# Expert stage of a hybrid decoder layer: token rows gathered as quarters and turned by VectorE, index copies on VectorE

## The reference

```python
def hier_moe(h, ...):                     # h: 2048 x 1024
    # top-1 of 4 groups, top-2 of the 8 experts in it: two assignments and two gates per token
    # assignments sorted by expert, each expert's rows padded to blocks of 128 (MOE_BLOCK)
    def expert_block(args):
        xb, e = args                      # xb: 128 rows of h, e: their expert
        hid = jax.nn.silu(xb @ w_gate[e]) * (xb @ w_up[e])   # 1024 -> 512
        return hid @ w_down[e]                               # 512 -> 1024
    out = lax.map(expert_block, (rows.reshape(n_blocks, 128, -1), block_e)).reshape(n_rows, -1)
    return segment_sum(out[dest] * gate, token)
```

## Time and profile before

| | |
|---|---|
| median of 3 runs | 2221.45 us |
| the runs | 2222.25, 2213.61, 2221.45 us |
| profiled execution: time / span | 2212.72 / 2211.1 us |
| busy: PE, PEld, DVE, ACT, POOL | 90%, 76%, 64%, 49%, 24% |
| TensorE clock granted, mean over the span | 0.954 |
| blocks in the expert stage (gate matmuls 392, eight per block and kind) | 49 |
| expert stage, from the first gate matmul to the last down split | 1244 to 2143 us of the span |

### The profile page before, as it was taken

The page is one execution under the profiler, slowest core; times in us unless marked ns, Lnnn a source line. Parts: engine busy times, 40 slices in busy tenths (PEclk is TensorE's granted clock), DMA queues, the critical chain, the costliest instruction groups (busy, mean ns, idle before and its releaser), DMA issues. The chain is left out here.

```text
span 2211.1 us, 32053 instructions
## 1 busy us (share of the span) xinstructions
PE 1996.7 (90%) x10153; PEld 1672.5 (76%) x10154; DVE 1415.3 (64%) x2368; ACT 1072.4 (49%) x1591; POOL 525.4 (24%) x637
## 2 busy tenths in 40 slices
PE   6999999886898988969996699999999999999970
PEld 5887888785687878858885588888888888888860
DVE  4675687466797887945556675675568755546344
ACT  4322211224377787753223364665567655545433
POOL 2000111241000000000000254454445545344430
PEclk9999999998899999989997699999999999999995
DMA  8675986835435323024335588797889978667637
GB/s 263 218 228 196 327 288 223 262 133 124 123 69 125 76 69 67 1 84 167 134 134 200 196 309 281 255 331 273 283 277 387 348 268 304 188 229 238 218 85 314
DMA packets 170121, 458.37 MB, mean 207 GB/s; under 512 B 19872, under 2 KB 69104, under 8 KB 144432
## 3 DMA queue, kind: packets, MB, share of 16 engines
q1 hardware_dynamic: 122896, 285.30, 37.4%
q0 software_dynamic: 31008, 138.37, 20.5%
q10 hardware_dynamic: 16128, 33.56, 4.3%
HBM read 342.08 MB, written 115.10 MB: 207 GB/s over the span
## 5 line engine op out<-in xcount | busy, mean ns | idle before, releaser
L2215 DVE TENSOR_TENSOR w_down_lo<-w_down_raw,w_down_hi 128x2048 fp32r<-128x2048 f32 x64 | 144.1, 2289 | 124.5 <-ACT w_down_hi L2152 123.0
L2299 PE MATMUL m_bank<-w_down_hi,hidden_T_hi 128*128 128x512 f32 x392 | 160.4, 409 | 6.8 <-DVE w_down_lo L2215 6.8
L2215 DVE TENSOR_TENSOR w_gate_lo<-w_gate_raw,w_gate_hi 128x2048 fp32r<-128x2048 f32 x63 | 141.6, 2289 | 38.8 <-ACT w_gate_hi L2152 32.4
L2278 PE MATMUL m_bank<-w_gate_hi,rows_T_hi 128*128 128x512 f32 x392 | 156.5, 399 | 6.4 <-DVE rows_T_lo L2220 3.9
L2278 PE MATMUL m_bank<-w_up_hi,rows_T_hi 128*128 128x512 f32 x392 | 158.8, 405 | 0.0
L2279 PE MATMUL m_bank<-w_gate_lo,rows_T_hi 128*128 128x512 f32 x392 | 156.1, 398 | 0.0
L2280 PE MATMUL m_bank<-w_gate_hi,rows_T_lo 128*128 128x512 f32 x392 | 156.0, 398 | 0.0
L2215 DVE TENSOR_TENSOR w_up_lo<-w_up_raw,w_up_hi 128x2048 fp32r<-128x2048 f32 x64 | 146.2, 2287 | 15.1 <-ACT w_up_hi L2152 15.1
L2300 PE MATMUL m_bank<-w_down_lo,hidden_T_hi 128*128 128x512 f32 x392 | 155.4, 396 | 0.0
L2280 PE MATMUL m_bank<-w_up_hi,rows_T_lo 128*128 128x512 f32 x392 | 154.8, 395 | 0.0
L2279 PE MATMUL m_bank<-w_up_lo,rows_T_hi 128*128 128x512 f32 x392 | 154.5, 394 | 0.0
(11 more groups left out here) (424 smaller groups left out, 5288.3 us busy)
## 6 DMA issues: line engine op xcount, KB each, us to landing
w_gate_raw<-in_w_gate_dram SPq DMA_DIRECT2D x64, 1024.0 KB
w_down_raw<-in_w_down_dram POOLq DMA_DIRECT2D x64, 1024.0 KB
w_up_raw<-in_w_up_dram SPq DMA_DIRECT2D x64, 1024.0 KB, 8.2
hT_d<-hT_parts SPq DMA_DIRECT2D x32, 512.0 KB, 5.2
hT_parts<-hT_d SPq DMA_DIRECT2D x32, 512.0 KB, 9.0
k_parts<-kT_d SPq DMA_DIRECT2D x64, 256.0 KB, 8.5
u_tok<-in_x_dram SPq DMA_DIRECT2D x16, 512.0 KB, 5.8
qT_d<-qk_out ACTq DMA_DIRECT2D x32, 256.0 KB, 3.8
```

Of the source, the lines that this page charges most:

```text
L2215: dve.tensor_tensor(wlo[w][:, halves[i]], raw[w][:, halves[i]], whi[w][:, halves[i]], ALU.subtract).then_inc(lo_done[w], 1)
L2278: pe.matmul(to[:], xh[:, k], whi[w][:, c], start=k == 0, stop=False)
L2299: pe.matmul(DN[h][:], hh[:, k], whi[2][:, part(k)], start=k == 0, stop=False)
```

## The change

A block's rows are gathered by four indirect DMAs in place of one. `h2` is seen as 1 KB quarter rows, and the DMA number `r` fills columns `256r` to `256r+255` of `rows_in`: partition `32f+i` gets quarter `f` of the token in slot `32r+i`. VectorE then turns 32x32 blocks (`turn`, two instructions of 128x512), which puts column numbers on partitions and slots along the free axis, in the new SBUF tile `rows_T`. The high and low parts of the rows are made from this tile. Blocks 0 and 1 keep the old way.

TensorE loses the 8 transposes of each iteration and the wait for `x_in`, and gets, once, four small matmuls that spread the token numbers over the partitions (`PI`). VectorE gets, once, `part_rows`, and in each iteration two `turn`, one `part_index`, two `slot_index` and waits for `x_in`, `out_st` and `gate_in`. GpSimd loses all index copies and two of its three small adds. ScalarE's wait for `u_done` moves ahead of the rows' high parts, which now wait for `turned`.

```diff
+    def pause(self, pool, ones, by=1):
+        pool.tensor_tensor(self.paused[:], ones[:, 0:1], ones[:, 1:2], ALU.add).then_inc(self.pauses, by)
+
+    def gather_parts(self, pool, d):
+        for r in range(PARTS):
+            pool.indirect_dma_start(self.x[:, r * PART:(r + 1) * PART], None, d["h2"].rearrange("r (f c) -> (r f) c", f=PARTS),
+                                    bass.IndirectOffsetOnAxis(ap=self.part_idx[:, r:r + 1], axis=0)).then_inc(self.x_in, 16)
...
             def _(pool):
-                def gather_gate(b, count):
-                    pool.tensor_copy(gate_idx[:], gate_ids[:, bass.ds(b, 1)]).then_inc(gate_set, 1)
-                    pool.wait_ge(gate_set, count)
-                    pool.tensor_tensor(hold[:], ones[:, 0:1], ones[:, 1:2], ALU.add)
+                def gather_gate():
                     pool.indirect_dma_start(gate[:], None, d["gates"], ...).then_inc(gate_in, 16)
-                def add_rows(b, count, used):
+                def add_rows(set_by, used, pauses):
+                    pool.wait_ge(store.pauses, pauses)
+                    pool.wait_ge(slot_ready, set_by)
                     pool.wait_ge(d_used, used)
-                    pool.tensor_copy(to_idx[:], ids[:, bass.ds(b, 1)]).then_inc(to_set, 1)
-                    pool.wait_ge(to_set, count)
-                    pool.tensor_tensor(hold[:], ones[:, 0:1], ones[:, 1:2], ALU.add)
+                    store.pause(pool, ones)
                     pool.indirect_dma_start(d["x1"], ..., out[:], None, compute_op=ALU.add).then_inc(out_st, 16)
...
                 with pool.Fori(0, later(pool) - 1) as j:
-                    pool.wait_ge(xT_psum, 2 * j + 6)
-                    gather(j + 3)
-                    add_rows(j, j + 1, 2 * j + 4)
-                    gather_gate(j + 1, j + 2)
+                    pool.wait_ge(store.pauses, 2 * j + 2)
+                    pool.wait_ge(turned, 2 * j + 2)
+                    pool.wait_ge(part_ready, j + 2)
+                    store.pause(pool, ones)
+                    store.gather_parts(pool, d)
+                    add_rows(2 * j + 3, 2 * j + 4, 2 * j + 3)
+                    gather_gate()
                     # the down weights' loads follow, as before
...
             # ScalarE
+                def rows_hi(h, want):
+                    act.wait_ge(turned, want)
+                    act.activation(xh[:, 4 * h:4 * h + 4], xT[:, 4 * h:4 * h + 4], ACT.Copy).then_inc(xh_done, 1)
...
-                    rows_hi(0, 2 * j + 5)
-                    rows_hi(1, 2 * j + 6)
+                    act.wait_ge(u_done, j + 2)
+                    rows_hi(0, 2 * j + 1)
+                    rows_hi(1, 2 * j + 2)
                     with where_below(nc, act, now, order):
-                        act.wait_ge(u_done, j + 2)
                         split_hi(1, order, 0)
                     out_half(0, j)
...
             # VectorE
+                def rows_lo(h, want):
+                    dve.wait_ge(xh_done, want)
+                    dve.tensor_tensor(xl[:, 4 * h:4 * h + 4], xT[:, 4 * h:4 * h + 4], xh[:, 4 * h:4 * h + 4],
+                                      ALU.subtract).then_inc(xl_done, 1)
+                def turn(h):
+                    dve.transpose(xT[:, 4 * h:4 * h + 4].rearrange("p k (r i) -> p r k i", r=PARTS),
+                                  x[:].rearrange("p (r j k) -> p r k j", r=PARTS, k=KT)[:, :, 4 * h:4 * h + 4]).then_inc(turned, 1)
+                def part_rows():
+                    # memset; copies into pick (128x512), ids_f (128x64), quad_i; shift; copy into quad
+                    dve.wait_ge(part_psum, 1)
+                    dve.tensor_scalar(part_ids[...], PI[...], float(PARTS), quad[:, 0:1], ALU.mult, ALU.add).then_inc(part_set, 1)
+                    dve.wait_ge(part_set, 1)
+                    part_index(2)
+                def part_index(b):
+                    dve.tensor_copy(store.part_idx[:], part_ids[:, bass.ds(b * PARTS, PARTS)]).then_inc(part_ready, 1)
+                def slot_index(b, of_rows):
+                    # one copy of 128x1 into to_idx (of_rows) or gate_idx, then_inc(slot_ready, 1)
...
                 split_lo(1, 0, 1)
+                part_rows()
                 split_lo(2, 0, 0)
                 split_lo(2, 0, 1)
...
                         split_lo(0, order, 1)
+                    dve.wait_ge(x_in, 64 * j + 96)
+                    dve.wait_ge(xl_done, 2 * j + 4)
+                    turn(0)
+                    turn(1)
+                    part_index(j + 3)
                     hidden(j + 1)
                     rows_lo(0, 2 * j + 5)
                     rows_lo(1, 2 * j + 6)
+                    dve.wait_ge(out_st, 16 * j + 16)
+                    slot_index(j, True)
+                    dve.wait_ge(gate_in, 16 * j + 16)
+                    slot_index(j + 1, False)
...
             # TensorE
                 product(G, 0, g_done)
+                pe.wait_ge(pick_set, 2)
+                for r in range(PARTS):
+                    last = pe.matmul(PI[:, r * NBLK:(r + 1) * NBLK], pick[:, r].rearrange("p f i -> p (f i)"), ids_f[:], start=True, stop=True)
+                last.then_inc(part_psum, 1)
...
                     product(U, 1, u_done)
-                    pe.wait_ge(x_in, 16 * j + 48)
-                    rows_T(0)
-                    rows_T(1)
                     down(j, before)
```

More of the change, by code:

```diff
@@ L43 @@
 NBLK = 64
+PARTS = 4
+PART = D // PARTS
+QUAD = P // PARTS
 MIN_BLK = 2 * SEQ // P
@@ L2056, in source, with experts @@
         return a[("w_gate", "w_up", "w_down")[w]][0, e].rearrange("o (p k) n -> p (o k n)", k=k)[:, self.halves[i]]
-def experts(nc, ident, ones, ids, gate_ids, meta, store, a, d):
+def experts(nc, ident, ones, const, ids, gate_ids, meta, store, a, d):
     with ExitStack() as ctx:
@@ L2063, in experts @@
         sem = ctx.enter_context(phase_semaphores(nc))
-        bank = [ctx.enter_context(nc.psum_tensor(f"m_bank{i}", [P, BANK], F32)) for i in range(7)]
-        G, U, XT, HT, DN = bank[0], bank[1], bank[2:4], bank[4], bank[5:7]
+        bank = [ctx.enter_context(nc.psum_tensor(f"m_bank{i}", [P, BANK], F32)) for i in range(8)]
+        G, U, XT, HT, DN, PI = bank[0], bank[1], bank[2:4], bank[4], bank[5:7], bank[7]
         FT = FF // P
@@ L2076, in experts @@
         x_in = store.x_in
-        gate_in, to_set, gate_set = (sem(n) for n in ("slot_gate_in", "to_idx_set", "gate_idx_set"))
+        gate_in, part_ready, slot_ready = (sem(n) for n in ("slot_gate_in", "part_idx_set", "slot_idx_set"))
         g_done, u_done, d_done, silu_done, hid_done = (sem(n) for n in ("g_done", "u_done", "d_done", "silu_done", "hid_done"))
-        xT_psum, xh_done, xl_done, hT_psum = (sem(n) for n in ("rT_psum", "rT_hi_done", "rT_lo_done", "hidT_psum"))
+        xT_psum, turned, xh_done, xl_done, hT_psum = (sem(n) for n in ("rT_psum", "rows_turned", "rT_hi_done", "rT_lo_done", "hidT_psum"))
+        pick_set, part_psum, part_set = (sem(n) for n in ("row_of_quad_set", "part_ids_psum", "part_ids_set"))
         with nc.Block() as block:
@@ L2139, in _ @@
                 end = later(pool)
-                add_rows(end - 1, end, 2 * end + 2)
-                gather_gate(end, end + 1)
-                add_rows(end, end + 1, 2 * end + 4)
+                add_rows(2 * end + 1, 2 * end + 2, 2 * end)
+                gather_gate()
+                add_rows(2 * end + 2, 2 * end + 4, 2 * end + 1)
                 final = place(pool, end - 1)
@@ L2230, in hidden_lo @@
                     dve.tensor_tensor(hl[:], HT[:].rearrange("p (k t) -> p k t", k=FT), hh[:], ALU.subtract).then_inc(hl_done, 1)
+                slot_index(0, False)
                 split_lo(0, 0, 1)
                 split_lo(1, 0, 0)
[L2234 to L2235 removed]
+                first_rows_lo(0, 1)
+                first_rows_lo(1, 2)
                 split_lo(1, 0, 1)
+                part_rows()
                 split_lo(2, 0, 0)
@@ L2264, in _ @@
                 end = later(dve)
+                dve.wait_ge(out_st, 16 * end + 16)
+                slot_index(end, True)
                 hidden_lo(end + 2)
@@ L2447, in hybrid_layer @@
             route(nc, ident, ones, logits, const, ids, gate_ids, meta, store, a, d)
-            experts(nc, ident, ones, ids, gate_ids, meta, store, a, d)
+            experts(nc, ident, ones, const, ids, gate_ids, meta, store, a, d)
         finish(nc, a, d, out)
```

52 lines of the change are left out of this document (36 added, 16 removed).

## The result

| | before | after |
|---|---|---|
| median | 2214.41 us (5 runs) | 2233.91 us (5 runs: 2232.27 to 2241.92) |
| profiled execution: time / span | 2212.72 / 2211.1 us | 2233.5 / 2231.9 us |
| gathers of rows, mean of one | 1.04 us x49 | 1.56 us x192 and one whole |

The ratio is 1.0084, with a 95% interval of 1.0057 to 1.0111: slower by 0.8%, where 2193 was forecast and 2223 was the end of the range. All ratios here are of undisturbed executions; one each of e1 and e2, and one of the kernel before beside them, took 2896 to 4100 us and is left out of its ratio.

A forecast was written before the change was run, and what follows sets the result against it. PE was taken as sole limit in 34 iterations, with three resources nearly as long in full ones. The terms -38.9 + 5.0 + 4.0 + 3.0 - 0.3 gave -27 us; forecast 2193 us, range 2176 to 2223.

The forecast's parts named there:

- TensorE's transposes: Row transposes leave PE's stream in 48 iterations: 0.81 us each, 38.9 us in all, a block passing in 17.34 us.
- The turn at 0.60 us: Each 128x512 turn on VectorE was priced like a subtraction of its shape: 0.60 us, bounds 0.30 to 1.20.
- The room in gate-and-up iterations: Slack before the next gate product: 2.68 us, 0.5 left after the change, hiding turns up to 0.85 us each.
- rival 2: Slow turns of 1.2 us lengthen gate-and-up and full iterations: -9 us in all, 2212; chance 0.13.
- first turn 0.60: The one turn counted in VectorE's 10.03 us part of the full iterations' loop, at 0.60 us.
- ScalarE's order: Rows' high parts wait for the turn, closing a 17.9 us loop in nine full iterations: +5.0 us.
- GpSimd and DMA, +4 us: Late down loads from four gathers, together with full DMA in full iterations: +4 us, bounds 0 and 18.
- uncovered: about 1 us: Down loads issued 4.2 us later but wanted 3 us later in full iterations, leaving about 1 us uncovered.
- The rule on two SBUF operands: VectorE instructions with two SBUF inputs delay GpSimd: two gathers, some 1.2 us more before down loads; left out.
- The start, +3.0: The index table waits for TensorE before the first down splits, delaying the second expert: +3.0 us, bounds 2 and 6.
- Rival 3: GpSimd's gathers and add, pausing for VectorE's splits, become the full iterations' loop: about +32 us, 2253; chance 0.15.
- the prediction's signs of being wrong: Turns over 0.85 us, four 2.8 us gathers with PE idle over 2, VectorE awaiting `x_in`, or clock below 1.00.

The follow-up runs named there:

- e1: The changed kernel with each VectorE turn cut to half of its columns; 2215.68 us, 0.9998 of the kernel before.
- e2: The changed kernel with one gather of whole rows in place of four of quarters; 2212.51 us, 0.9990 of the kernel before.
- e13: The changed kernel with turns reading neighbouring columns and the loop's low parts taking their second operand from a zeroed PSUM bank; 2186.78 us.
- e5: The changed kernel with turns that read 32 neighbouring columns in place of every eighth; 2207.91 us.
- e9: The changed kernel with the loop's weight low parts taking a PSUM bank of zeros as second operand instead of the high part; 2211.07 us.
- e10: The changed kernel with a second, reordered copy of h2 stored and gathered, so turns read neighbouring columns and results are kept; 2214.33 us.
- e3: The changed kernel with half turns and one gather of whole rows; 2189.23 us, 0.9881 of the kernel before.
- e7: The changed kernel with turns and index copy ahead of the gate splits and part of the index table's making behind the first down splits; 2235.66 us.

## Why the prediction was wrong, step by step

From the first gate product to the last lie 47 of the 48 blocks, so its sum there was -26.1 (-38.1 + 5.0 + 4.0 + 3.0); measured was +16.0. The gap of 42 us, by the kinds of interval: full 21.3 (forecast -11.3 + 9.0 = -2.3, measured +19.0), gate and up 13.5 (-13.0, +0.5), down only 7.1 (-13.0, -5.9), start 0.4. Taking both wrong prices away (e13) gave back 19.9, 14.9 and 7.2.

- *TensorE's transposes, 0.81 us a block:* right. The interval without splits is 17.23 us after, forecast 17.34; gate-and-up ones too, once the turn is short (17.25).
- *The turn at 0.60 us:* the first failed step. It is 1.17 (e5: 0.69 when it reads neighbouring columns), at the upper bound of 1.20. The choice went by the shape of the nearest row, a subtraction that reads neighbours; the stride was named as what speaks for 1.20, and then outweighed. The room in gate-and-up iterations was worked out as enough for 0.85 a turn; with 1.17 they are 0.8 us over 17.34 (rival 2 had 0.6). In the loop of the full iterations the prediction counted one turn, "first turn 0.60". At 1.17 both stand in it: the first on DVE, the second as ACT's wait of 0.45 us between the two rows' high parts (1677.00 above). In the run of six, behind its first, e9 with the long turns has intervals of 18.90 to 18.98 us, e13 with the short ones mostly 17.95: 0.95 us, twice the 0.48. The mean of all full intervals got 0.76 shorter (e10).
- *ScalarE's order, a loop of 17.9 us:* right in mechanism and size where both prices are taken away: 17.95 in e13, with ACT's and DVE's parts as worked out. (e3's 17.97 is a mean over blocks of 17.27 to 19.15 us and comes near it by chance.)
- *GpSimd and DMA, +4 us:* the second failed step. The place was right: the down loads were put at 12.9 us behind the gate product, and came at 10.4 to 14.0, 13.3 ahead of the longest block. What they cost was not: "uncovered: about 1 us". In a run of full iterations they land at 1684.4 and 1689.0, 11.0 and 15.0 us after their issue, ACT waits 4.3 us, and the interval is 23.76 us. Two of the 14 are like this (the other took 23.88), and the nine that follow a full one have a mean of 20.3 us where 17.9 + 4.0 / 9 = 18.3 was forecast. The delay also spills into the down-only iterations that follow and into DVE's waits for gathered rows (52.9 us), both counted as nothing. Slow landing alone is not the cause: in e2 such loads land 11.4 to 14.1 us after an issue at 10.5, and ACT waits 2.5 us in the whole stage. e9 removes most of the loss: 9.0 us from the full, 7.5 from the down-only and 3.0 from the gate-and-up intervals. The rule on two SBUF operands was given 1.2 us for two gathers, and left out of the sum.
- *The start, +3.0:* right, 3.4 (19.92 against 16.53). The table's wait for TensorE is 5.34 us in DVE's timeline.
- *Rival 3* had the mechanism of the second step, at 22 us for a full iteration and 19.9 as the point of decision. Measured are 19.63 over the 14, with the slow turn in it. *Rival 2* had the first at 2212. Neither alone gives 2234. The range left out rival 3 and had no case of both, while nothing made them exclude each other.

The granted clock fell too, as the prediction's signs of being wrong had it. PE idled 2.50 us before 1693.51, and from 1694.10 to 1697.30 it was granted 0.50, the lower of its two levels (1.2 GHz), and again from 1704.40 to 1707.60. The mean over the block of 23.76 us is 0.93, over those of 17.95 in e13 1.00. What this costs by itself is not separated; an estimate from the first of these stretches is 1.6 us at most, half of its 3.20.

```profile
1694.10:1697.30 3.20, 3.20 (x9) 2.55 (x8) 3.20 (x3) 1.73 (x1) 0.36 (x1) 0.50 1.02 334
```

## What to carry to other kernels

Price a new operation by the row with its access pattern, not its shape, and when two prices are each uncertain, work out the case in which both are at their bad end. Before giving GpSimd more DMAs to issue, look at what VectorE runs beside them: subtractions with two SBUF operands, one after the other, can hold up an indirect DMA until they end (8.61 us in e7). A load that a queue issued late cost nothing that shows in a lone full iteration here, and several microseconds where such iterations follow each other.

## What the runs showed of the hardware

- A 32x32-block transpose of 128x512 float32 on VectorE takes 0.69 us from neighbouring columns and 1.17 us at a stride of 8.
- The issue of an indirect DMA takes 0.95 to 1.0 us alone, and up to 8.61 us beside four 128x2048 subtractions of two SBUF tensors back to back (e7); with one operand in PSUM the mean is 1.04 us (e9), where it was 1.56. Moving DVE's work to get the index sooner made it worse (2.01).
- The same stages ahead of the experts ended up to 6.4 us apart in the profiled executions of the kernels that leave them as they were (stage start at 1244.1 to 1250.5 us).
- TensorE's granted clock was 1.00 from 1659 to 1693 us, with a gap of 2.50 us before 1693.51, and 0.50 (1.2 GHz) from 1694.10 to 1697.30.
